# A state-space layer recast as runs of eight steps, with the modulation products beside it in one stage

## The reference, cut to what matters

```python
u = (h @ w_in).reshape(bsz, seq, 32, 16)               # 32 groups of 16 channels
# a = exp((lam_re + i lam_im) dt), one complex number for each group and each of 64 states
bu = einsum('bsgc,gpc->bsgp', u, bbar)                  # complex
x[t] = a * x[t-1] + bu[t]                               # associative_scan over 512 steps
y = real(einsum('bsgp,gcp->bsgc', x, c)) + d_skip * u
z = gelu(y); z = z * sigmoid(z @ w_glu); out = z @ w_out
...
mod_x = silu(c) @ w_ada + b_ada                         # 1024 x 6144
mod_c = silu(c_ctx) @ w_ada + b_ada
```

## Time and profile before

| | |
|---|---|
| median of 3 runs | 3481.39 us (3479.74 to 3483.93) |
| the profiled execution | 3478.96 us |
| its span, first to last instruction | 3477.1 us |
| mean granted TensorE clock | 0.934 |
| TensorE, VectorE, ScalarE, GpSimd busy | 3084.1, 2178.8, 1550.8, 561.3 us |

### The profile page before, as it was taken

The page is one execution under the profiler, slowest core; times in us unless marked ns, Lnnn a source line. Parts: engine busy times, 40 slices in busy tenths (PEclk is TensorE's granted clock), DMA queues, the critical chain, the costliest instruction groups (busy, mean ns, idle before and its releaser), DMA issues. The chain is left out here.

```text
span 3477.1 us, 39208 instructions
## 1 busy us (share of the span) xinstructions
PE 3084.1 (89%) x13624; PEld 2304.8 (66%) x13624; DVE 2178.8 (63%) x2502; ACT 1550.8 (45%) x1656; POOL 561.3 (16%) x458
## 2 busy tenths in 40 slices
PE   7776899989487999979996983999999999999995
PEld 2111687878356877844564763888888888888883
DVE  5696412344774213255366333899999999999994
ACT  2111322232153222232344222777777777777771
POOL 0263021000030220000120003112121121222221
PEclk9878899999688999999998995999999999999997
DMA  5500122221101222211000304999999999999993
GB/s 223 195 0 15 64 97 81 96 95 52 49 1 55 97 86 90 85 63 61 25 1 1 109 25 186 364 385 381 389 382 388 379 389 379 386 384 388 384 360 128
DMA packets 85539, 636.16 MB, mean 183 GB/s; under 512 B 10064, under 2 KB 10576, under 8 KB 22272
## 3 DMA queue, kind: packets, MB, share of 16 engines
q1 hardware_dynamic: 73888, 596.25, 44.7%
q0 software_dynamic: 10736, 37.24, 2.9%
q10 hardware_dynamic: 816, 1.34, 0.1%
HBM read 612.23 MB, written 22.62 MB: 183 GB/s over the span
## 5 line engine op out<-in xcount | busy, mean ns | idle before, releaser
L255 PE MATMUL banks<-arena_rounded,operand_rounded 128*128 128x512 f32 (+1 forms) x2512 | 994.8, 396 | 45.8 <-DVE operand_rounded L412 36.3
L2149 DVE TENSOR_TENSOR arena_rounded<-arena,arena_rounded 128x2048 fp32r<-128x2048 f32 x420 | 950.9, 2285 | 93.7 <-ACT arena_rounded L2145 93.6
L256 PE MATMUL banks<-arena_rounded,operand_rounded 128*128 128x512 f32 (+1 forms) x2512 | 982.1, 391 | 0.0
L2145 ACT ACTIVATE arena_rounded<-arena 128x2048 fp32r<-128x2048 f32 x420 | 801.7, 1918 | 211.6 <-PE banks L257 139.4
L257 PE MATMUL banks<-arena_rounded,operand_rounded 128*128 128x512 f32 (+1 forms) x1952 | 763.8, 391 | 0.0
L255 PEld LDWEIGHTS banks<-arena_rounded,operand_rounded 128*128 128x128 f32 x2512 | 478.1, 190 | 142.5 <-DVE operand_rounded L412 38.6
L256 PEld LDWEIGHTS banks<-arena_rounded,operand_rounded 128*128 128x128 f32 x2512 | 478.4, 190 | 95.4
L244 DVE TENSOR_TENSOR arena_rounded<-arena,arena_rounded 128x2048 fp32r<-128x2048 f32 x75 | 171.9, 2292 | 566.8 <-ACT arena_rounded L240 566.8
L257 PEld LDWEIGHTS banks<-arena_rounded,operand_rounded 128*128 128x128 f32 x1952 | 372.5, 191 | 77.3
L240 ACT ACTIVATE arena_rounded<-arena 128x2048 fp32r<-128x2048 f32 x75 | 143.4, 1913 | 433.2 <-PE banks L257 407.1
L255 PE MATMUL banks<-operand_rounded,arena_rounded 128*128 128x512 f32 x576 | 227.7, 395 | 19.9 <-PEq L291 14.6
(11 more groups left out here) (367 smaller groups left out, 3701.5 us busy)
## 6 DMA issues: line engine op xcount, KB each, us to landing
arena<-in_gate SPq DMA_DIRECT2D x140, 1024.0 KB, 6.5
arena<-in_up SPq DMA_DIRECT2D x140, 1024.0 KB, 6.9
arena<-in_down SPq DMA_DIRECT2D x140, 1024.0 KB, 5.9
arena<-in_dense SPq DMA_DIRECT2D x62, 2048.0 KB, 7.7
arena<-routed SPq DMA_DIRECT2D x4, 2048.0 KB, 14.7
arena<-in_dense SPq DMA_DIRECT2D x6, 1024.0 KB, 5.0
resid<-in_x SPq DMA_DIRECT2D x1, 2048.0 KB, 5.0
small<-in_rows SPq DMA_DIRECT2D x4, 512.0 KB, 6.9
```

The lines of the kernel that those rows point to most:

```text
L255: nc.tensor.matmul(out, left[0], right[0], start=start, stop=False)
L256: nc.tensor.matmul(out, left[0], right[1], start=False, stop=False)
L2145: nc.scalar.activation(high[q % NHI], raw[:, q, :], ACT.Copy).then_inc(high_ready, 1)
L2149: nc.vector.tensor_tensor(low[q], raw[:, q, :], high[q % NHI].bitcast(F32), ALU.subtract).then_inc(low_ready, 1)
```

## The change

`ssm_parameters`, `ssm_tables` and `ssm_scan` become one stage, `ssm_scan`. The 512 steps are cut in 64 runs of 8. Within a run the answer to an input d steps back is a block-diagonal 128x128 product ("tap" d, 0 to 7) on `u`; across runs the state at a run's end is carried by a recurrence of 64 steps with the decay to the eighth power. The matrices for this (G = B times a to the power d, H = C times a to the power d) are built by VectorE, spread into block-diagonal form by ScalarE, turned and multiplied by TensorE. `gather(h)` sums each run's inputs into the state, four pairs on four row quarters; at the end the state at a run's start is spread over its eight steps, four pairs on four column quarters, in the banks to which the taps have been added.

The modulation products of a chunk go to four column quarters, two products each, on cleared banks; the copy takes all 128 partitions, and the turning is a product with a constant `sel` that adds the quarters. Their order over chunks is `ADA_ORDER`, and they are spread between the layer's steps. The raw matrices are stored without their zero halves (0.5 MB, before 1 MB). The core of the diff (the removed stages stand above; `...` leaves out parameters that are as before, names and layouts):

```diff
+ADA_ORDER = (0, 1, 3, 4, 2, 6, 7, 5, 9, 10, 8, 11)
...
+    chunk_order = [ada0, ada0 + 1, FIRST["ssm_in"]] + [ada0 + a for a in ADA_ORDER[2:]]
...
+            for n, c in enumerate(chunk_order):
+                sp.wait_ge(released, n + 1)
+                k.load_chunk(sp, c + NSLOT)
...
+            nc.gpsimd.memset(spare, 0.0).then_inc(zeroed, 1)
+            for g in grams:
+                nc.gpsimd.memset(g, 0.0).then_inc(zeroed, 1)
+            pool.wait_ge(u_product, WT)
+            nc.gpsimd.memset(taps, 0.0).then_inc(zeroed, 1)
...
+            def ada(n):
+                if n < 12:
+                    m = k.chunk(pe, ada0 + ADA_ORDER[n], NB)
+                    if n >= 2:
+                        pe.wait_ge(ada_copied, n - 1)
+                    for d in range(DT):
+                        q = d % 4
+                        i = nc.tensor.matmul(k.psum[32 * q:32 * q + 2, 4 + n % 2, :], k.silu_c[:, 2 * d:2 * d + 2], m[:, d, :],
+                                             start=(d < 4), stop=(d >= 4), tile_position=(0, 32 * q))
+                    i.then_inc(ada_done, 1)
+                    pe.wait_ge(ada_done, n + 1)
+                    pe.sem_inc(released, 1)
+                if n >= 1:
+                    pe.wait_ge(ada_copied, n)
+                    for f in range(4):
+                        col = 2 * (4 * ADA_ORDER[n - 1] + f)
+                        i = nc.tensor.matmul(mod_psum[:, col:col + 2], mod_rows[:, f * P:(f + 1) * P], k.cst("sel"),
+                                             start=True, stop=True)
+                    i.then_inc(ada_turned, 1)
...
+            def gather(h):
...
+                for i in (2 * h, 2 * h + 1):
+                    for part in range(2):
+                        at = 128 * (i % 2) + 64 * part
+                        for t in range(RUN):
+                            for q in range(4):
+                                rows = slice(32 * q, 32 * q + 32)
+                                m = nc.tensor.matmul(k.psum[:, q, at:at + NRUN], into[part][rows, i, RUN - 1 - t, :],
+                                                     in_runs[rows, i, :, t], start=(t == 0), stop=(t == RUN - 1))
...
+            pe.wait_ge(silu, 1)
+            pe.wait_ge(cleared, 1)
+            ada(0)
+            ada(1)
...
+            ada(2)
+            ada(3)
+            pe.wait_ge(u_copied, WT)
+            turn(0)
+            ada(4)
+            turn(1)
+            ada(5)
+            turn(2)
+            ada(6)
+            turn(3)
+            pe.wait_ge(g_kept_act, 8)
+            pe.wait_ge(g_kept_dve, 8)
+            gather(0)
+            ada(7)
+            ada(8)
+            pe.wait_ge(run_read, 4)
+            gather(1)
+            for n in range(9, 13):
+                ada(n)
+            pe.wait_ge(tap_kept, 16)
+            for i in (3, 0, 1, 2):
+                if i == 0:
+                    pe.wait_ge(mod_read, 1)
+                for d in range(RUN):
+                    nc.tensor.matmul(y_runs[:, i, :, d:RUN], taps[:, i, d, :], in_runs[:, i, :, 0:RUN - d],
+                                     start=(d == 0), stop=False)
+            for i in range(WT):
+                pe.wait_ge(states, 2 * (i // 2) + 2)
+                for t in range(RUN):
+                    for part in range(2):
+                        for q in range(4):
+                            m = nc.tensor.matmul(y_runs[32 * q:32 * q + 32, i, :, t], grams[part][:, 4 * i + q, t + 1, :],
+                                                 state[part][:, 4 * i + q, 0:NRUN], start=False,
+                                                 stop=(t == RUN - 1 and part == 1), tile_position=(0, 32 * q))
...
+            nc.scalar.activation(k.silu_c, k.col("cond"), ACT.Sigmoid).then_inc(silu_half, 1)
             nc.scalar.activation(v["dt"], k.col("log_dt"), ACT.Exp).then_inc(act_done, 1)
...
+            copy_ada(2)
+            act.wait_ge(zeroed, 4)
+            open_up_g(0)
+            copy_ada(3)
+            open_up_h(0)
+            keep(0)
+            open_up_g(1)
...
+            V.memset(k.psum[:, 4:6, :], 0.0).then_inc(cleared, 1)
+            dve.wait_ge(silu_half, 1)
+            V.tensor_tensor(k.silu_c, k.silu_c, k.col("cond"), ALU.mult).then_inc(silu, 1)
```

## The result

The changed kernel takes 3344.4 us (median of 4 runs, 3343.5 to 3348.0) beside 3481.4 us for the kernel before on the same chip: a ratio of 0.9608, with a 95% interval of 0.9591 to 0.9624. The forecast was 3364, so the direction and the range held and the point was 19.6 us too high. The profiled execution took 3347.98 us with a span of 3346.2, and its mean granted clock was 0.938.

The account below looks back on a forecast made before the run. It took a chain of 298 us, owned first by TensorE, then VectorE, as the bound. The layer's end moves from 322.6 to 205.2, 117.4 less: 3478.96 becomes 3361.6, plus 2.4 for the median: 3364 us, range 3322 to 3410.

Parts of the forecast that it names:

- TensorE's first product: Layer's start: modulation products wait for VectorE's operations to 31.3, a clearing of 1.1 us and silu 0.2; start at 32.7.
- end of `u`: Two modulation chunks of 3.4 and about 2.7 us first, then `u` from 40.0 to 67.7.
- first gather starts: After GpSimd's clearing to 71.3, the first opening and four rounds building G and H: last copy at about 103.
- second gather ends: Two gathers of 15.6 us each with two chunks between, from 103: ends at 140.0.
- taps start: After the last chunk's load lands at 152.5 and 3.5 us of its products and turning: 156.0.
- states start: After tap products of 15.4 us plus 2.5 for a half clock: 174.0.
- last state record ends: State outputs, 512 records at 0.061, take 31.2 us: end at 205.2, with the layer's gate following.
- The rounds: Four rounds building G and H, paced by VectorE at 9.2 us each; ScalarE 8.4, TensorE under 6.
- the rival with 12 us more of load: Layer's tail: last chunk's load runs beside two others, landing at 165 and not 152.5; 3376 us, chance 0.10.
- The first opening: Before the rounds: ScalarE's opening copies wait 3.6 us behind `u` for GpSimd's clearing of 4096 columns, to 71.3.
- cheap small records: Gathers and states: quarters overlap and issue does not pace; gathers 7.2 each, states near 13; 3329 us, chance 0.27.
- its own mechanism: Whole kernel: the forecast's timetable with small records at 0.061 us; 3345 to 3385, likeliest 3364, chance 0.57 together with the loads.

Follow-up runs that it names:

- one-quarter run: Changed kernel with all products of a modulation chunk writing the same two rows, on one quarter of the columns: 3399.7 us, ratio 0.9768 to the kernel before.
- order of chunks: Changed kernel with the modulation chunks reordered, so the one whose slot comes free last is not asked for last: 3331.1 us, ratio 0.9575 to the kernel before.
- open early: Changed kernel with ScalarE opening the first G without waiting for GpSimd's clearing of the taps: 3342.0 us, ratio 0.9604 to the kernel before.
- late clearing: Changed kernel with GpSimd clearing the two Gram tables only behind VectorE's phase columns, each in four pieces: 3338.2 us, ratio 0.9592 to the kernel before.
- quarter outermost: Changed kernel with the loop over the four quarters outermost in gathers and states: 3423.6 us, ratio 0.9836 to the kernel before.

## Why the prediction came out as it did

The timetable against the trace, in the forecast's own steps (us; the last column is what the step itself added):

| step | forecast | measured | step's error |
|---|---|---|---|
| TensorE's first product | 32.7 | 40.60 | +7.9 |
| end of `u` | 67.7 | 76.07 | +0.5 |
| first gather starts | 103 | 114.82 | +3.4 |
| second gather ends | 140.0 | 140.91 | -10.9 |
| taps start | 156.0 | 165.67 | +8.8 |
| states start | 174.0 | 183.62 | -0.1 |
| last state record ends | 205.2 | 194.78 | -20.0 |

**Right.** Four quarters run side by side: 1.90 us a chunk against 1.71 plus drain, and the one-quarter run pays 5.1 a chunk. The rounds are VectorE's, 9.44 us for 9.2, with one wait for the first opening. The last chunk waits for its load where the forecast put the wait, 7.27 us, asked for at 150.20 and used at 159.34; the rival with 12 us more of load did not come.

**Right by luck.** The tap products are 17.95 for 17.9, but at the full clock they are 16.3 (order of chunks) and not 15.4, and the half clock cost 1.7 and not 2.5. The first opening came 4.0 us behind `u` for the forecast's 3.6, but it waited for ScalarE's copy of the third chunk and not for GpSimd's clearing (open early). The time itself came near because two large errors cancelled, as the sum below shows.

**The start failed.** "so the exponential and with it VectorE's 17 operations come 1.5 us later, to 31.3" counted the instructions of VectorE's own list and did not look at GpSimd's, where the change had put clearings beside them. The late clearing gave the 7.6 us back. The Trainium skill ("SBUF — State Buffer", Who interferes with whom) has the rule: VectorE's second port pair is GpSimd's too, as an exclusive lock held for a whole instruction; and "VectorE: DVE Perf Modes" (Mode 2x_2P) has an fp32 operation with one source in SBUF use both ports, one with two sources not. The trace agrees: 4.04 and 3.87 us beside a clearing, for the one kind, 0.17 for the other.

**The small records were mis-sized.** "The most tightly packed records of the trace, 24 in 1.46 us, are 0.061 apart" took the spacing of records that stream 128 columns each as the price of an issue. It was their stream. Here 64 columns in four quarters need 0.054/4 = 0.0135, and the states run at 0.015. The prediction called itself failed if a gather or the states lasted half as long: the states took 11.2 us for 31.2 and the first gather 7.85 for 15.6, so by its own sign it failed here. The rival "cheap small records" (chance 0.27) named what came: 7.2, 7.2 and 13 us; measured 7.85, 12.2 and 11.2. What it lacked is a second limit behind the first (with both stops 512 state records take 0.022 each) and the half clock in the second gather. The run with the quarter outermost shows that it is the order of the loops that buys the pace, 3.3 times in a gather and 3.4 in the states at the full clock.

**The rounds were 3.4 us long.** The wait for the first opening ended 0.6 us later than forecast, three rounds took 0.7 more, and the last turning 2.1 more: it waited for ScalarE's last opening and then ran at the half clock (granted 0.52; 1.91 us for 1.07).

**The tail was late twice.** The two chunks before the last load ran at the half clock, 3.59 and 1.84 us for 1.90 and 1.02, so the slot came free 5.4 us late, 0.9 of it inherited; the load then took 9.1 us and not 7.7, and the last chunk with its turning and two copies 6.3 and not 3.5.

**The sum.** Errors of 20.6 us upward and 31.0 downward leave the layer 10.4 us shorter than forecast. With the small records as measured and all else as forecast, the sum would have been 3333, 11 us too low. The measured 3344.4 lies just below the 3345 to 3385 that the forecast gave its own mechanism, and inside the whole range, 3322 to 3410, which reaches half way to the cheap records. The other 9.2 us of the 19.6 are not of the mechanism: the spans differ by 3.2 more behind the layer, and the profiled execution was 3.6 above its median, where the forecast had set it 2.4 below.

## What to carry to other kernels

When a change puts a clearing on GpSimd, look at what VectorE runs beside it on one tensor and scalars; cut the clearing or move it. For small products let the array's quarters be the innermost loop, and mix the short ones with long ones, which took the stops away here. When two orders of the same products are compared, read the granted clock beside the times: half of what the gathers lost here was the clock. When the work above a ring of loads gets shorter, go through the order again: the chunk used last should not sit in the slot that is freed last, which was worth more (13 us) than any other repair here.

## What the runs showed of the hardware that was not expected

A VectorE scalar operation of 16 columns stood still for a whole GpSimd clearing, up to 4.04 us, and no longer than to the end of the running piece when it was cut (0.55 us). Records of 128x32 tiles on four quarters ran at 0.0149 us each for 268 records, then stopped 1.0 to 2.0 us, and again after 128 more. One quarter's records start as far apart with the three others beside it as without, 0.118 us for row tiles of 32x128 and 0.055 for column tiles of 128x32, so that four in turn give close to four times the pace. With one row quarter at a time the granted clock fell to 0.50 after 3.3 us without an idle moment and stayed there for the 37 us left of the gather (0.213 us between records); with one column quarter at a time it was 1.00 throughout.
